# Gathering an expert's rows one block ahead, and a column sum moved behind a projection, in a fp32 mixture-of-experts block

## What is computed

```python
c_act = silu(c)
mod = c_act @ w_ada + b_ada              # six vectors: shift, scale, gate for mixer and ffn
h = rmsnorm(x) * (1 + sc1) + sh1         # mixer
q, k, v, z = split(h @ w_in)             # z = (u, vv)
y_a = chunk_attention(q, k, v, rel_bias)
y_b = u * spatial(layernorm(vv))
x = x + gt1 * rmsnorm((sig(g_a) * (y_a @ w_a) + sig(g_b) * (y_b @ w_b)) @ w_out)
h = rmsnorm(x) * (1 + sc2) + sh2         # ffn: each row goes to 4 of 32 experts
for e in experts:                        # rows of expert e, gathered
    gu = rows @ w_gate_up[e] + b_gate_up[e]
    act = clamp(glu) * sigmoid(1.702 * glu) * (clamp(lin) + 1)
    y[rows] += gate * (act @ w_down[e] + b_down[e])
x = x + gt2 * rmsnorm(y)
```

## Time and profile before

| | |
|---|---|
| times of three executions | 1193.82, 1195.16, 1199.39 us; median 1195.16 |
| the profiled execution | 1199.1 us, its span 1196.8 us |
| TensorE busy | 1039.2 us (87%) |
| DMA moved | 464.91 MB, mean 388 GB/s |
| chain that ended last | PE 68%, DMA 20%, DVE 5%, issue 4% |
| gate-up matmuls (line 1539) | 387.2 us |
| down matmuls (line 1568) | 198.4 us, idle 52.8 us before them for DMA |
| gather (line 1503) | 72.3 us, idle 39.6 us before them |
| combine (line 1484) | 75.5 us |

### The profile page before, as it was taken

The page is one execution under the profiler, slowest core; times in us unless marked ns, Lnnn a source line. Parts: engine busy times, 40 slices in busy tenths (PEclk is TensorE's granted clock), DMA queues, the critical chain, the costliest instruction groups (busy, mean ns, idle before and its releaser), DMA issues.

```text
span 1196.8 us, 21565 instructions
## 1 busy us (share of the span) xinstructions
PE 1039.2 (87%) x8299; PEld 503.4 (42%) x8301; DVE 295.1 (25%) x813; ACT 179.7 (15%) x453; POOL 31.3 (3%) x54
## 2 busy tenths in 40 slices
PE   4979999978786999899989998999899989697966
PEld 3837888533341343334333433343334333233322
DVE  4644655232110112111211121112111211111112
ACT  3212240121110101101110111111111111001102
POOL 1001001210000000000000000000000000000000
PEclk9989999978896999999999999999999999788977
DMA  9897944989999969999999999999999999999995
GB/s 351 320 374 293 350 172 153 422 343 412 423 425 424 390 277 427 423 428 425 425 427 425 424 425 428 424 405 426 425 427 412 428 423 426 427 422 427 425 424 230
DMA packets 61484, 464.91 MB, mean 388 GB/s; under 512 B 5900, under 2 KB 10060, under 8 KB 28568
## 3 DMA queue, kind: packets, MB, share of 16 engines
q1 hardware_dynamic: 60736, 462.47, 93.7%
q0 software_dynamic: 336, 1.07, 0.2%
q10 hardware_dynamic: 392, 1.09, 0.2%
HBM read 462.50 MB, written 2.11 MB: 388 GB/s over the span
## 4 chain that ended last, share of the span: by engine, by line
PE 68%; DMA 20%; DVE 5%; issue 4%; ACT 2%; DVEq 0%; SPq 0%; POOL 0%; ACTq 0%
PE pp L1539 26%; DMA arena<-in_w_down_dram 17%; PE pp L1568 14%; PE pp L1503 5%; PE pp L1325 5%; DMA arena<-in_w_ada_dram 3%; PE pp L1247 3%; PE pp L1338 2%; PE po L1400 2%; PE pp L1512 2%; PE po L1484 2%; PE pp L1518 1%; PE pp L1257 1%; ACT work L720 1%; DVE work L1094 1%
## 5 line engine op out<-in xcount | busy, mean ns | idle before, releaser
L1539 PE MATMUL pp<-arena,work 128*32 128x256 f32 (+1 forms) x3840 | 387.2, 458 | 20.1 <-ACT work L720 20.1
L1539 PEld LDWEIGHTS pp<-arena,work 128*32 128x32 f32 (+1 forms) x3840 | 169.0, 120 | 222.6 <-issue 140.5
L1568 PE MATMUL pp<-arena,work 128*32 128x256 f32 (+1 forms) x1920 | 198.4, 458 | 52.8 <-DMA arena<-in_w_down_dram 52.8
L1568 PEld LDWEIGHTS pp<-arena,work 128*32 128x32 f32 (+1 forms) x1920 | 77.0, 121 | 153.4 <-issue 68.1
L1091 DVE TENSOR_SCALAR work<-pp 128x128 f32<-128x128 f32 (+1 forms) x74 | 25.0, 338 | 418.9 <-PE pp L1539 418.9
L1503 PE MATMUL pp<-h_sb,work 128*32 128x256 f32 (+1 forms) x480 | 72.3, 528 | 39.6 <-issue 35.2
L723 ACT ACTIVATE work<-work 128x128 f32<-128x128 f32 (+1 forms) x74 | 25.9, 350 | 416.2 <-DVE work L1091 416.2
L1085 DVE COPY work<-pp 128x256 f32<-128x256 f32 (+1 forms) x37 | 19.4, 526 | 246.4 <-PE pp L1503 246.4
L1484 PE MATMUL po<-work 64*128 64x512 f32 x304 | 75.5, 615 | 1.2 <-ACT work L739 1.2
L1503 PEld LDWEIGHTS pp<-h_sb,work 128*32 128x32 f32 (+1 forms) x480 | 23.2, 132 | 84.0 <-issue 78.6
L1325 PE MATMUL pp<-arena 128*128 128x256 f32 x256 | 57.1, 382 | 0.0
(11 more groups left out here) (224 smaller groups left out, 627.6 us busy)
## 6 DMA issues: line engine op xcount, KB each, us to landing
arena<-in_w_gate_up_dram SPq DMA_DIRECT2D x128, 2048.0 KB, 27.6
arena<-in_w_down_dram SPq DMA_DIRECT2D x32, 2048.0 KB, 32.3
arena<-in_w_down_dram SPq DMA_DIRECT2D x64, 1024.0 KB, 19.4
arena<-in_w_ada_dram SPq DMA_DIRECT2D x11, 2048.0 KB, 14.2
arena<-in_w_in_dram SPq DMA_DIRECT2D x4, 2048.0 KB, 19.2
arena<-in_w_gate_dram SPq DMA_DIRECT2D x4, 2048.0 KB, 12.6
arena<-in_w_out_dram SPq DMA_DIRECT2D x2, 2048.0 KB, 10.6
arena<-in_w_ada_dram SPq DMA_DIRECT2D x2, 1024.0 KB, 13.4
```

The costliest lines, as they stand in the source:

```text
L1539: mm = t_.matmul(pp[j * m:(j + 1) * m, UP[hh], 0:w].rearrange("p (s f) -> p s f", s=2), hgT[:, at:at + m], gu_w[slot][:, k, :, r * PAIR:(r ...
L1568: mm = t_.matmul(pp[j * m:(j + 1) * m, UP[0], 0:w], actT[:, at:at + m], wd[:, j * w:(j + 1) * w], start=(n == 0), stop=(n == KD - 1))
```

## The change

Three parts.

1. In the mixer, `page_rows("vv")` now stands ahead of `modulation_sum(2)` on TensorE. On VectorE the product with gain1, which needs that sum, moves behind the statistics of vv.
2. A block's rows are gathered and transposed during the down pass of the block before it: the gather after four of the eight steps, the transposes after six. They are always made in the wide form, 64 rows, whichever the block is; a narrow block reads half of hgT. VectorE makes sel and selg for the next block, and copies the gathered rows, at the end of the block; ScalarE copies hgT there too. For the first block this is done ahead of the loop, and VectorE computes ranks and the first sel before the table of block counts. The first of combine's four matmuls moves to the start of the block, ahead of the biases; the other three stay where they were. So the block's first matmul now waits for y_sb.
3. TensorE loads the next block count and wide count in the down pass, after its fourth step, in every block; before, it loaded them once per expert, between the experts.

```diff
             modulation(2)
-            dve.wait_ge(s_adasum, 3)
-            dve.wait_ge(s_gain[1], 16)
-            v.tensor_tensor(gain1, gain1, flat2(mod_bank(2)), ALU.mult).then_inc(s_mod_v, 1)
             dve.wait_ge(s_projev, 9)
             modulation(3)
...
                 v.bn_aggr(meanvar[:, t, :], stats[:, t, :]).then_inc(s_mv, 1)
+            dve.wait_ge(s_adasum, 3)
+            dve.wait_ge(s_gain[1], 16)
+            v.tensor_tensor(gain1, gain1, flat2(mod_bank(2)), ALU.mult).then_inc(s_mod_v, 1)
...
-            modulation_sum(2)
             page_rows("vv")
+            modulation_sum(2)
...
+            def gather(it, bank):
+                pe.wait_ge(s_sel, it)
                 for t in range(TT):
                     for j in range(2):
+                        mm = t_.matmul(pp[j * TB:(j + 1) * TB, bank, :], sel[:, t, :], h_sb[:, t, j * 512:(j + 1) * 512],
+                                       start=(t == 0), stop=(t == TT - 1))
+                mm.then_inc(s_hg, 1)
+
+            def turn_rows(it):
+                pe.wait_ge(s_hgs, it)
+                for i in range(4):
+                    mm = t_.transpose(pp[:, TURN, i * P:(i + 1) * P],
+                                      hg[:, i // 2 * PAIR + i % 2:(i // 2 + 1) * PAIR:2], ident[:])
+                mm.then_inc(s_turn, 1)
...
                 pe.wait_ge(s_bgu[slot], landed * 2)
-                pe.wait_ge(s_sel, it)
...
+                combine(it, ((0, 0),))
...
-                combine(it)
+                combine(it, ((0, 1), (1, 0), (1, 1)))
...
                 for n, k in enumerate(order):
+                    if n == 2:
+                        pe.wait_ge(s_aTev, halves[1])
+                    if n == 4:
+                        next_place()
+                        pe.wait_ge(s_selTev, it)
+                        gather(it + 1, TOKS)
+                    if n == 6:
+                        turn_rows(it + 1)
                     if k in (4, 6):
                         pe.wait_ge(s_dhi[k // 2 - 2], dhi_landed)
...
+                    def next_place():
+                        place = pe.snap((i * 2 + (slot + 1)) % NEXP, min_val=0, max_val=NEXP - 1)
+                        pe.reg_mov(next_nb, pe.value_load(nblk_i[0:1, bass.ds(place, 1)], min_val=1, max_val=NBLK))
+                        pe.reg_mov(next_wide, pe.value_load(wide_i[0:1, bass.ds(place, 1)], min_val=0, max_val=NBLK))
...
                     act.wait_ge(s_selT, it + 1)
                     a.copy(selgT.rearrange("p t n -> p (t n)"), pp[:, TOKS, 0:TT * P]).then_inc(s_selTev, 1)
+                    act.wait_ge(s_turn, it + 1)
+                    a.copy(hgT, pp[:, TURN, :]).then_inc(s_turned, 1)
                     act.wait_ge(s_y, it)
```

More of the change, by code:

```diff
@@ L1098, in block_of, with blocks @@
                     v.tensor_tensor(x_sig, x_lin, x_sig, ALU.mult).then_inc(s_actv, 1)
-            def select(places, e):
-                dve.wait_ge(s_tabs, 1)
-                for t in range(TT):
-                    ins = v.tensor_scalar(sel[:, t, :], places, rank[:, t, e], None, ALU.is_equal)
-                ins.then_inc(s_sel, 1)
-                for t in range(TT):
-                    for c in range(2):
-                        ins = v.tensor_scalar(selg[:, t, c, :], places, rank[:, t, e], gate_tab[:, t, e], ALU.is_equal,
-                                              ALU.mult)
-                ins.then_inc(s_selg, 1)
-            def blocks(nb, wide, e):
+            def blocks(nb, wide, n):
                 with dve.Fori(0, nb) as b:
@@ L1144, in _ @@
             with dve.Fori(1, NEXP) as n:
-                nb, wide, e = place_of(bass.ds(n, 1))
-                blocks(nb, wide, bass.ds(e, 1))
+                nb, wide = place_of(bass.ds(n, 1))
+                blocks(nb, wide, n)
             dve.wait_ge(s_x1b, 16)
@@ L1278, in _ @@
             mm.then_inc(s_proj, 1)
+            page_rows("vv")
             modulation_sum(2)
[L1280 removed]
             page_T("u")
```

101 lines of the change are left out of this document (56 added, 45 removed).

## The result

The changed kernel takes 1210.72 us, the median of four runs (1209.73 to 1213.15), where the kernel before takes 1196.18 in the runs beside it. The ratio is 1.0127, with a 95% interval of 1.0099 to 1.0155: it is slower, by 14.5 us. The prediction was 1197, with 1187.5 to 1206, so it was wrong. The profiled execution took 1209.73 us, with a span of 1207.4; that is 10.6 us more than the span of before, and these 10.6 us are what the traces can account for.

A forecast was written before the change was run, and what follows sets the result against it. The weights' DMA stream bounds the experts' stage, TensorE the mixer. Mixer -8.6, first block +3.3, expert 5 +0.3, four two-block experts +5.2, tail +1.5 sum to +1.7 us; on the median 1195.16 that gives 1197 us, range 1187.5 to 1206.

The forecast's parts named there:

- The mixer: Mixer: vv ahead of the sum ends u earlier and moves all behind it, a gain of 8.6 us.
- Expert 5: Expert with two wide blocks: 2 us more of lower clock in its first pass, s_dhi_free 0.3 us later.
- Step 1: Block's front: a quarter of combine costs 0.48 us; the shorter rest saves 0.4 us in narrow blocks, nothing in wide.
- Step 2: Expert 9's front: combine and biases at twice their warm time, and 0.3 us for a later rise of the clock.
- Step 3: Down pass: the two count loads cost 0.8 us in a narrow block, 0 in a wide one.
- the prediction's L: Time of the two count loads in the down pass: 0.8 us narrow (0.3 to 1.34), 0 wide (0 to 0.5).
- The four two-block experts: Later experts with two blocks: s_dhi_free 1.3 us later in each, 5.2 us in all.
- (b): Rival: uncovered loads in narrow down passes (about 1.1 us or more) make TensorE the bound; 1206 us, chance 0.17.
- The first block: Start of the experts' stage: gate-up 1.0 us later, then the longer down pass; cost 3.3 us (1 to 6).
- The tail: Last block: its down pass gathers for a block that isn't there; cost 1.5 us.
- (a): Rival: the down pass's additions are hidden and the mixer's gain stays; 1188.5 us, chance 0.33.
- (c): Rival: the sum moved in the mixer brings nothing, a page or VectorE being late; 1205.5 us, chance 0.08.

The follow-up runs named there:

- vv_only: The kernel before with only the mixer's edit (vv ahead of the third modulation's sum, gain1 product behind the statistics): 1187.55 us, ratio 0.9921.
- split_only: The kernel before with only combine's first matmul moved to the block's front, behind the gather: 1204.64 us, ratio 1.0071.
- pair_front: The changed kernel with combine cut between its pairs, two matmuls ahead of gate-up and two behind: 1194.41 us, ratio 0.9982.
- busy_wait: The changed kernel with four unused bf16 matmuls ahead of the wait for y_sb: 1195.04 us, ratio 0.9996.
- late_busy: whole_combine with loads and gather behind the sixth down step, row transposes behind the last, and four filler matmuls before the y_sb wait: 1192.29 us, ratio 0.9971.
- whole_combine: The changed kernel with combine whole at its old place, a one-column matmul waiting for y_sb at the front: 1192.23 us, ratio 0.9957.
- loads_between: The changed kernel with the two loads of the counts back between the experts: 1218.36 us, ratio 1.0188.
- whole_busy: The changed kernel with combine whole at its old place and four filler matmuls ahead of the wait for y_sb: 1189.01 us, ratio 0.9946.
- pair_busy: pair_front with four filler matmuls while TensorE waits for y_sb: 1190.74 us, ratio 0.9962.
- half_gather: The changed kernel with rows 128 to 255 never gathered, so its output differs: 1193.05 us, ratio 0.9968.

## Why the prediction was wrong

**What held.** The mixer: 8.6 us forecast, 9.1 in the trace, 9.0 by vv_only. Expert 5: 0.3 forecast, 0.5 seen, in part by luck. I had put 2 us more of lower clock into its first pass; that one lost 0.55 us (16.48 against 15.93) and its second, where I had put none, 1.7 (15.65 against 13.95). (Redone, the sum gives 0.2: T + 63.2 before, not 63.1.) The gather's 1.94 us, the transposes' 0.65 to 0.7, y_sb's 1.24 and 0.7: all as costed. That DMA would no longer be dry at 91 us held too (383 GB/s there, against 12 before).

**Step 1 that failed: the price of a quarter of combine.** "A quarter of combine, 0.48 us (1.99 / 4)" divides a group by its count. The group consists of two pairs that run side by side, so a quarter costs a half: 1.05 us, and the rest is not shorter by 0.4 us but by nothing. That is 0.57 + 0.4 us too little for each narrow block and 0.57 for a wide one. split_only shows the price alone, pair_front that it is the pair. The Trainium skill says that matmuls in different row groups of the array run concurrently ("TensorE: Matmul & The Clock Gate", "Part 3: Packing small matmuls — row/col tiling"); this trace agrees, with 1.05 us for one and 1.06 for two. The row already said it, had I read its form: "64*128", half of the array's rows.

**Step 2 that failed: the clock.** I allowed 0.3 us for a later rise in expert 9. The traces show 1.7 us in such a pass (15.65 against 13.95). And I took the lower level for combine and biases at the front, where the trace has the upper one for both: the fall comes behind them, inside the pass. busy_wait and late_busy give the clock's price with all else left in place, 15.7 and, though not fully mended, 19.8 us on their kernels; the forecast had neither. whole_combine shows when it is paid: only where TensorE sets the pace.

**Step 3: the loads.** Taken 0.8 us in a narrow block, measured 0.34; 0 in a wide one, as forecast. The Trainium skill gives a floor of about 600 ns for a tensor_load ("DMA: Bandwidth & Descriptors", "Latency and other measured facts"); by that the estimate was 1.2 us for the two. No run here shows a load's own time, but the visible part of the two together, 0.34 us, is well under that. That error was in the other direction. What the prediction lacked is that between the experts the loads also cost the clock: loads_between is 7.6 us slower (its biases at expert 9 already run at the lower level), where the prediction's L makes it about 4 us faster.

**The cycle, with these terms.** By the prediction's own figures TensorE's work filled a cycle of 119.6 + (4.2 - 3.7) = 120.1 us; the 120.5 to 121 that it named came from the late issue instead. Expert 9's front piece adds 0.1, that of the four other blocks 0.57 each, combine's rest 0.4 in each of three narrow blocks, the loads -0.46 in each of these, the clock 1.4, the biases at the upper level -0.8: 122.9 us, which is what the trace has. This is an account from rows of this cycle; the runs show its two large terms, not each of them. The four two-block experts cost +13.1 us instead of +5.2, which is most of the miss. It is also why each microsecond counted: at 120.1 us the prediction stood half a microsecond past the point at which TensorE takes over from the stream, and costed the stage as if it were still before it. Rival (b) says that TensorE takes over from loads of about 1.1 us on, because there the extra work passes 3.7 us; by the prediction's own 4.2 us at 0.8 it had passed already, and does so from 0.63 us on.

**The first block.** Forecast +3.3, seen +4.7: gate-up lost 2.5 us instead of 1.0, since the first lone matmul took 2 us at the lower clock and 1.82 us of "issue" stood ahead of it, at the entry into the loop. Of the entry I had taken 0.9 us, and up to 3.7 from the earlier trace rows. The Trainium skill says that a taken branch out of the fetched pages forces a fetch, an instruction-fetch stall ("Runtime: NRT & Kernel Launch", "Instruction fetch mechanics"). The trace fits that in its direction: there is idle "issue" ahead of combine's front matmul in the first block (1.82 us) and in the third (2.81 us, at 297.80), and in none after them. No run isolates a fetch, and the 3.7 us did not come. From gate-up to the release it was 2.2 us, forecast 2.34.

**The tail.** Forecast +1.5, seen +0.4: the last pass took 8.68 us, against 9.52 before, and the loads 0.36 us instead of 0.8. (Redone, the terms of that forecast add up to 1.4.)

**The rivals.** (b) had the right bound, TensorE, and the wrong lever. It was tied to loads of 1.1 us or more; they were 0.34, and the bound came all the same, by the pairs and the clock. So the range ended at 1206, where both together lead to 1211; with either one taken away the kernel is at 1192 to 1195. (a) has its number in vv_only, 1187.55, but not as it was meant: the additions are not hidden. (c) fell. The range was too narrow for a reason: each bound was varied alone, around a point next to a change of bound, and the clock had no bound of its own.

## What to carry to other kernels

Before costing a part of a group as its share, read the form of the row: here two matmuls on the two halves of the array's rows took the time of one, and a cut inside such a pair paid the pair's time twice; cut between pairs. When a change brings TensorE near the stream's pace, write the cycle of both down and cost every microsecond per block in full beyond the crossing; and where it puts a wait of a microsecond ahead of a long pass, add the lower clock's price, or fill the wait with work, which recovered 15.7 and 19.8 us on the two kernels that TensorE bounds, and 3.2 and 3.7 on the two in which combine was mended already (whole_busy, pair_busy). An edit whose gain stands alone (here the mixer's, 9 us) is worth measuring apart from its companions, which here cost 22.

## What the runs showed of the hardware

- One matmul on 64 of the 128 rows takes 1.05 us until the next group starts (changed kernel, split_only), two on the two halves take 1.06 us together (pair_front), four in a row 1.92 (before) and three 1.91 (changed kernel).
- Equal idle times did not give equal clocks, and the lone matmul does not decide it either. Behind 1.24 us of idle time and a lone half-array matmul, the pass at expert 9 takes 15.65 us in the changed kernel and 13.95 in half_gather, and that at expert 11 of the changed kernel 13.95. Behind the same idle time and a pair, all fourteen wide passes of pair_front take 13.96 us in the mean (195.4 in all). With neither, behind the same wait and a one-column matmul, whole_combine has passes of both kinds (13.95 at 503.75, 15.65 at 573.76). What decides is not settled: no run varied what stands on TensorE ahead of a pass with the idle time and all else held. What the runs do show is that filling the waits raises the clock: 195.4 us for all wide passes in busy_wait, 214.1 without the filling.
- The two loads in the down pass show as 0.34 us of idle time on TensorE in a narrow block and none in a wide one; between two experts the idle time ahead of the first matmul was 1.73 us instead of 1.24.
- Idle time without a releaser that the profile shows stood ahead of combine's front matmul in two of the 37 blocks only, the first (1.82 us) and the third (2.81 us); the group row has 4.6 us of "issue" in all.
